# Four channel sums per round as two rounded products each, and the key norm at the end of the round before

## The reference

```python
kk = k * k_k.reshape(hs)
kk = kk / jnp.maximum(jnp.linalg.norm(kk, axis=-1, keepdims=True), 1e-12)      # key norm
...
var = jnp.mean(jnp.square(y - mu), axis=-1, keepdims=True)                      # variance of the output
y = (y - mu) * lax.rsqrt(var + B_LN_EPS) * ln_g.reshape(hs) + ln_b.reshape(hs)
y = y + jnp.sum(r * k * r_k.reshape(hs), axis=-1, keepdims=True) * v            # bonus
...
oa = _rmsnorm(_hgrn2(qa, fa, ia, lb), hg_norm.reshape(A_HEADS, A_HEAD_DIM))     # norm of the HGRN2 output
```

## Time and profile before

| | |
|---|---|
| runs before | 1185.59, 1187.63, 1187.63 us; median 1187.63 |
| the profiled execution | 1185.91 us, span from first to last instruction 1184.1 us |
| granted TensorE clock | 0.996 of full speed |
| TensorE busy | 1148.4 us (97%) |
| VectorE, Pool, ScalarE busy | 760.6 us (64%), 631.1 us (53%), 446.6 us (38%) |

### The profile page before, as it was taken

One profiled execution on the slowest core, in us unless ns is written; L12 is line 12 of the kernel. 1 busy time (PEld: TensorE's weight loads), 2 busy tenths in 40 slices (PEclk: granted clock), 3 DMA queues, 4 the chain that ended last, 5 costly groups with the idle time before them and its releaser, 6 DMA issues.

```text
span 1184.1 us, 31046 instructions
## 1 busy us (share of the span) xinstructions
PE 1148.4 (97%) x12076; PEld 907.4 (77%) x12076; DVE 760.6 (64%) x1339; ACT 446.6 (38%) x844; POOL 631.1 (53%) x594
## 2 busy tenths in 40 slices
PE   7899999999999999999999999998999999999996
PEld 4678877777788788777887878886677777778884
DVE  7874684675666746755766541638568686968637
ACT  5452343342533432434335410225234344453224
POOL 5553452442444524434444667876557474749872
PEclk9999999999999999999999999999999999999999
DMA  6221221221221212212112143333223222313331
GB/s 199 75 70 48 55 70 35 66 55 41 63 56 55 65 40 62 66 38 65 56 46 72 48 148 114 95 98 89 80 64 89 72 83 68 89 63 91 106 89 71
DMA packets 46890, 87.38 MB, mean 74 GB/s; under 512 B 5824, under 2 KB 7104, under 8 KB 46656
## 3 DMA queue, kind: packets, MB, share of 16 engines
q1 hardware_dynamic: 44496, 81.04, 23.4%
q10 hardware_dynamic: 2288, 4.72, 1.2%
HBM read 83.65 MB, written 2.10 MB: 72 GB/s over the span
## 4 chain that ended last, share of the span: by engine, by line
PE 80%; DVE 10%; ACT 3%; issue 2%; DVEq 0%; ACTq 0%
PE psum L398 77%; ACT mix L1175 2%; DVE mix L1733 2%; PE psum L1079 1%; DVE mix L2398 1%; PE psum L550 1%; DVE mix L2385 1%; DVE mix L2376 1%; DVE mix L2396 1%; DVE h_split L1737 1%; DVE mix L2486 0%; DVE psum L1853 0%; DVE psum L2287 0%; PE psum L712 0%; PE psum L548 0%
## 5 line engine op out<-in xcount | busy, mean ns | idle before, releaser
L398 PE MATMUL psum<-h_split,w_hi 128*128 128x512 f32 x2320 | 751.0, 405 | 17.5 <-DVE h_split L1733 8.2
L398 PEld LDWEIGHTS psum<-h_split,w_hi 128*128 128x128 f32 x2320 | 421.7, 189 | 124.8 <-issue 32.1
L352 POOL TENSOR_SCALAR w_hi<-w_raw 128x512 fp32r<-128x512 f32 x290 | 211.1, 728 | 492.8 <-PE psum L398 348.0
L398 PE MATMUL psum<-h_split,w_lo 128*128 128x512 f32 x1160 | 454.8, 392 | 0.0
L354 POOL TENSOR_TENSOR w_lo<-w_raw,w_hi 128x512 fp32r<-128x512 f32 x290 | 408.3, 1408 | 24.2
L1175 ACT ACTIVATE mix<-psum 128x512 f32<-128x512 f32 (+4 forms) x292 | 140.8, 496 | 384.6 <-PE psum L398 252.8
L398 PEld LDWEIGHTS psum<-mix 64*64 64x64 f32 (+3 forms) x8256 | 229.0, 138 | 70.6 <-issue 48.8
L398 PE MATMUL psum<-mix 64*64 64x64 f32 (+5 forms) x8256 | 270.1, 236 | 5.4 <-issue 2.4
L398 PEld LDWEIGHTS psum<-h_split,w_lo 128*128 128x128 f32 x1160 | 218.5, 188 | 47.7
L1175 ACT ACTIVATE mix<-mix 128x512 f32<-128x512 f32 (+3 forms) x256 | 131.4, 547 | 118.7 <-DVE mix L2268 48.0
L1853 DVE COPY_PREDICATED mix<-mask,psum 128x128 f32<-128x128 uint8 (+1 forms) x192 | 82.0, 469 | 44.2 <-PE psum L398 41.8
(11 more groups left out here) (136 smaller groups left out, 666.9 us busy)
## 6 DMA issues: line engine op xcount, KB each, us to landing
w_raw<-wall SPq DMA_DIRECT2D x290, 256.0 KB, 2.6
mix<-xT SPq DMA_DIRECT2D x4, 512.0 KB, 6.9
mix<-xT ACTq DMA_DIRECT2D x1, 2048.0 KB, 8.0
out<-mix SPq DMA_DIRECT2D x7, 256.0 KB, 2.5
mix<-pT ACTq DMA_DIRECT2D x2, 512.0 KB, 3.6
mix<-lru_w ACTq DMA_DIRECT2D x4, 256.0 KB, 3.1
mix<-w2a ACTq DMA_DIRECT2D x16, 32.0 KB, 2.3
mask<-mask_u SPq DMA_DIRECT2D x1, 432.0 KB, 7.5
```

What stands on the lines that cost most here:

```text
L352: pool.tensor_scalar(w_hi[:, slot, :, :], w_raw[:, slot, :], 1.0, 0.0, ALU.mult, ALU.add).then_inc(sem["w_hi"], 1)
L398: return pe.matmul(o, lhsT, rhs, start=start, stop=stop, skip_group_check=True)
```

## The change

Each of the four sums of a round becomes two products of fp32r type: the rounded (high) half of the operand, then the low half, both against rounded constants, added in the same bank. The last round's variance sum stays one fp32 matmul.

- The high halves are made by ScalarE (a second Square or a Copy with an fp32r output), the low halves by Pool (full minus high), at fixed places between its splits: output square behind the fourth unit of a round, bonus product behind the fifth, variance behind the fifteenth, keys behind the sixteenth. Pool's loop now runs over rounds, with 16 splits written out.
- The three halves that share `sum_split[:, 0]` (key, output square, bonus) take turns: ScalarE waits for the sum before.
- The key sum on TensorE moves from the beginning of a round to the end of the round before, between t(7) first half and `hg_level` 6; VectorE's clamp moves to the place ahead of `states`; ScalarE's Ln and Exp of it move ahead of the decay Exps. `low_rank`, which writes the same bank, waits for the clamp.
- In the last round the HGRN2 norm moves to the middle of tile 3.
- To make room in SBUF, `n_add`, `s_all`, `t2` and the odd layer's `osig` now share memory with other tiles. Two semaphores that nobody waits for are gone.

```diff
+        sum_split = sb("sum_split", [P, 2, 2, T], F32R)
+        sum_const = sb("sum_const", [P, 2, P], F32R)
+        ones_r, bones_r = sum_const[:, 0, :], sum_const[:, 1, :]
...
+            def key_low(r):
+
+                pool.wait_ge(sem["sum_hi"], count("sum_hi", r, 0))
+                pool.tensor_tensor(sum_split[:, 0, 1, :], t1, sum_split[:, 0, 0, :].bitcast(F32), ALU.subtract).then_inc(sem["sum_lo"], 1)
...
+            def variance_low(r):
+
+                pool.wait_ge(sem["rw_dsq"], count("rw_dsq", r))
+                pool.tensor_tensor(sum_split[:, 1, 1, :], y_sq, sum_split[:, 1, 0, :].bitcast(F32), ALU.subtract).then_inc(sem["dsq_lo"], 1)
+
+            pool.wait_ge(const_loaded, 64)
+            pool.tensor_scalar(sum_const[:, :, :], fconst[:, 1:3, :], 1.0, 0.0, ALU.mult, ALU.add)
...
+            with pool.Fori(1, EV_ROUNDS) as i:
+                for g in range(groups):
+                    for slot in range(SLOTS):
+                        split_unit(i * groups + g, slot)
+                        if g == 0 and slot == 3:
+                            output_square_low(i - 1)
+                        elif g == 1 and slot == 0:
+                            bonus_low(i - 1)
+                        elif g == 3 and slot == 2:
+                            variance_low(i - 1)
+                key_low(i)
...
+            def sum_products(o, of, pair):
+
+                mm(o, of, sum_split[:, pair, 0, :], True, False)
+                return mm(o, of, sum_split[:, pair, 1, :], False, True)
...
             def key_norm(r):
-                pe.wait_ge(sem["rw_ksq"], count("rw_ksq", r))
+                pe.wait_ge(sem["sum_lo"], count("sum_lo", r, 0))
+                sum_products(R0[:, :], bones_r, 0).then_inc(sem["rw_ssq"], 1)
...
             def bonus(r):
-                pe.wait_ge(sem["rw_rk"], count("rw_rk", r))
-                pe.wait_ge(sem["rw_m1"], count("rw_m1", r))
-                mm(R0[:, :], bones, t2).then_inc(sem["rw_bon"], 1)
...
             def hg_norm(r):
-                pe.wait_ge(sem["hg_sq"], count("hg_sq", r))
-                mm(H0[:, :], ones, hk).then_inc(sem["hg_ssq"], 1)
+                pe.wait_ge(sem["sum_lo"], count("sum_lo", r, 1))
+                sum_products(H0[:, :], ones_r, 0).then_inc(sem["hg_ssq"], 1)
...
                 t(7, 0, 4)
+                key_norm(i)
                 hg_level(i, 6)
...
                 low_rank(r)
-                part_tile(EV_ROUNDS, 3, 0, KC)
-                key_norm(r)
+                part_tile(EV_ROUNDS, 3, 0, 4)
                 hg_norm(r)
+                part_tile(EV_ROUNDS, 3, 4, KC)
                 head_var(r - 1)
                 bonus(r)
...
             def out_squares(r):
                 act.wait_ge(sem["rw_yc"], count("rw_yc", r))
...
+                    if not is_first(r):
+                        act.wait_ge(sem["rw_var"], count("rw_var", r - 1))
+                    f(by_parity(sum_split[:, 1, 0, :].rearrange("p (c t) -> p c t", c=RC)),
+                      psum[:, 2:4, 256:512].rearrange("p g (c t) -> p g c t", c=4), ACT.Square).then_inc(sem["rw_dsq"], 1)
...
+            def bonus_high(r):
+                act.wait_ge(sem["rw_rk"], count("rw_rk", r))
+                act.wait_ge(sem["hg_ssq"], count("hg_ssq", r))
+                f(sum_split[:, 0, 0, :], t2, ACT.Copy).then_inc(sem["sum_hi"], 1)
...
                     act.preload_act_table_set("natural_log_exp_and_others")
+                    key_scale(r)
...
                     if is_first(r):
                         decay_rates()
-                    act.wait_ge(sem["rw_m1"], count("rw_m1", r))
-                    f(t1, t1, ACT.Ln).then_inc(sem["rw_ln"], 1)
-                    act.wait_ge(sem["rw_ln"], count("rw_ln", r))
-                    f(t1, t1, ACT.Exp, bias=bias[:, 2:3], scale=-0.5).then_inc(sem["rw_rn"], 1)
+                    bonus_high(r)
...
-                f(t1, wk, ACT.Square, scale=cur_e[:, K_K:K_K + 1]).then_inc(sem["rw_ksq"], 1)
+                f(t1, wk, ACT.Square, scale=cur_e[:, K_K:K_K + 1])
+                if pair:
+                    act.wait_ge(sem["rw_bon"], count("rw_bon", r))
+                f(sum_split[:, 0, 0, :], wk, ACT.Square, scale=cur_e[:, K_K:K_K + 1]).then_inc(sem["sum_hi"], 1)
...
                 f(hk, H1[:, :], ACT.Square).then_inc(sem["hg_sq"], 1)
+                act.wait_ge(sem["rw_ssq"], count("rw_ssq", i))
+                f(sum_split[:, 0, 0, :], H1[:, :], ACT.Square).then_inc(sem["sum_hi"], 1)
...
                 if pair:
                     decay_sums(r)
-                    key_norm(r)
                     operands(r)
                     read_operands(r)
...
                 masked(i, 7)
+                key_norm(i)
                 states(i)
```

More of the change, by code:

```diff
@@ L50 @@
 SLOTS = 4
+MIX = 26700
 OUT_EARLY = (0, 1, 4, 5, 6, 2, 3, 7)
@@ L174, in place @@
             used[0] += width
-            assert used[0] <= 28800, used[0]
+            assert used[0] <= MIX, used[0]
             return mix[:, at:at + width]
@@ L195, in trunk @@
         shift = place(T + 8)
-        t1, t2, w_a = (place(T) for _ in range(3))
+        t1, w_a = (place(T) for _ in range(2))
+        t2 = kr[:, 0, :]
         cum = place(RC * (RL + 1)).rearrange("p (c t) -> p c t", c=RC)
@@ L505, in key_norm, with head_var, bonus @@
             def key_norm(r):
-                pe.wait_ge(sem["rw_ksq"], count("rw_ksq", r))
-                pe.wait_ge(sem["rw_sw"], count("rw_sw", r))
[L508 to L515, removed]
-                mm(R1[:, :], bones, y_sq).then_inc(sem["rw_var"], 1)
-            def bonus(r):
-                pe.wait_ge(sem["rw_rk"], count("rw_rk", r))
-                pe.wait_ge(sem["rw_m1"], count("rw_m1", r))
-                mm(R0[:, :], bones, t2).then_inc(sem["rw_bon"], 1)
+                pe.wait_ge(sem["sum_lo"], count("sum_lo", r, 0))
+                sum_products(R0[:, :], bones_r, 0).then_inc(sem["rw_ssq"], 1)
+            def head_var(r):
+                if isinstance(r, int) and r == EV_ROUNDS - 1:
+                    pe.wait_ge(sem["rw_dsq"], count("rw_dsq", r))
+                    pe.wait_ge(sem["rw_s"], count("rw_s", r, 5))
+                    last = mm(R1[:, :], bones, y_sq)
+                else:
+                    pe.wait_ge(sem["dsq_lo"], count("dsq_lo", r))
+                    pe.wait_ge(sem["rw_av"], count("rw_av", r + 1))
+                    last = sum_products(R1[:, :], bones_r, 1)
+                last.then_inc(sem["rw_var"], 1)
+            def bonus(r):
+                pe.wait_ge(sem["sum_lo"], count("sum_lo", r, 2))
+                pe.wait_ge(sem["rw_sw"], count("rw_sw", r))
+                sum_products(R0[:, :], bones_r, 0).then_inc(sem["rw_bon"], 1)
             def token_rows(r, n, head):
```

62 lines of the change are left out of this document (40 added, 22 removed).

## The result

The changed kernel takes **1197.72 us** in the median of four runs (1194.62 to 1198.89), against 1186.61 us of the kernel before beside it (1184.02 to 1187.63): ratio 1.0092 [1.0069, 1.0115], so 11 us slower. Six further runs of the changed kernel in a later series gave 1197.29 us, against 1186.14 us of 18 runs of the kernel before, ratio 1.0085 [1.0069, 1.0102]. The direction was forecast; the size (4.6 us) was less than half of it, and the time lies 0.7 us above the range. The profiled executions differ by 13.0 us (1198.89 to 1185.91).

A forecast was written before the change was run, and what follows sets the result against it. TensorE, busy 97%, was taken as the bound, with VectorE close behind in the head. Round terms 0.45 - 1.15 + 4.5 + 0.8 gave +4.6 us on the 1187.6 median: 1192.2 us, range 1180 to 1197.

The forecast's parts named there:

- The sum: Whole kernel: round 0 +0.45, round 1 -1.15, rounds 2 to 7 +4.5, last round +0.8, in total +4.6 us.
- the last round, put at +0.8 us: Before the first embedding tile: Pool's bonus half delays the bonus sum and the embedding halves; tile 0.8 us late (0.6 to 1.2).
- the regular rounds: Rounds 2 to 7: each loses 0.3 us in the head and 0.455 for the key sum at its end, +4.5 together.
- A sum costs 0.88 on TensorE, two products 0.455: TensorE's sums: each one made two rounded products saves 0.425 us; 31 of them take 13.2 us off TensorE.
- Pool holds VectorE, and the head gives the saving back: Round's head: Pool's added subtractions delay VectorE, so TensorE loses its whole 2.15 us saving and 0.3 more.
- The walk: VectorE and Pool in the head, step by step with hold prices: gating ends at 568.1 (566.41 before), masked copies 578.3 (577.48).
- Where TensorE waits: Just before the first inverse step: TensorE waits for the bonus, then gate product and masked copies, some 2 us per round.
- Round 1 at -1.15 us: Round 1: VectorE's 2.51 us wait ahead of the gate lets TensorE keep 1.6 us; with the key sum back, -1.15.
- The first rival: Masked copies end in time and TensorE stays the only bound: only the last round's loss remains, -10.2, 1177.4 us; chance 0.12.
- it evens out: The head gains 0.45 us, what the key sum at the round's end costs: no change, 1187.7 us; chance 0.16.
- serialises in full: Every Pool instruction of the head holds VectorE fully: head +1.3 us a round, +11 in total, 1198.6 us; chance 0.10.

The follow-up runs named there:

- version 1: Changed kernel without Pool's low halves of output square and bonus; each sum's second product rereads the high half (wrong values): 1180.51 us.
- version 3: Changed kernel with the output norm's and bonus's sums back as single fp32 sums, without halves: 1181.49 us.
- 2: Changed kernel with VectorE's gating of q moved ahead of the read operands: 1199.74 us.
- 9: Changed kernel; in the last round alone, output norm's and bonus's sums are fp32 without halves, the norm's sum behind the whole partial tile: 1192.39 us.
- version 11: Changed kernel with output norm's and bonus's sums in fp32 and, in the last round, the norm's sum behind the whole partial tile: 1178.99 us.
- version 4: Changed kernel with all four sums back in fp32, keeping only the early key norm: 1186.47 us.
- version 5: Changed kernel with the output norm's sum back in fp32; the bonus's low half stays on Pool: 1190.87 us.

## Why the prediction was right and wrong

The mechanism of the head (Pool's halves hold VectorE, and TensorE waits for it) was right, the place of the wait was not. The sum failed at two steps: the last round, put at +0.8 us, cost 3.9, and the sum had no term for half clock and issue waits, which the traces put at 4.6 us in the even rounds. Luck is in it too: the regular rounds were put 2.3 us too high, which hid a part of the rest.

- **A sum costs 0.88 on TensorE, two products 0.455: right.** By the starts of equal products a regular round's head gets shorter at the sums by 2.05 us in the changed trace (0.88 + 3 x 0.425 = 2.15 forecast), round 1's, which has no variance sum, by 1.65 (1.7 forecast), and each round gets 0.47 back at its end.
- **Pool holds VectorE, and the head gives the saving back: right, and shown** by 1 and 3. The walk put the gating at 568.1, 13.18 us after the scan's start; measured 13.20. The four multiplies ahead of it end within 0.1 us of the walk too, so this is no luck. Behind it the walk was too slow: the gate product ends 21.08 us after the scan's start, not 21.6. The price of a whole subtraction (1.16 us of VectorE's busy time) is in 1. The Trainium skill (GPSIMD Engine Reference, Specifications) speaks of shared SBUF interfaces for VectorE instructions with two SBUF inputs; the scan (1.24 to 1.63) and the multiplies lengthen, the gating from PSUM stays at 0.68: it agrees.
- **Where TensorE waits: wrong.** The step "It finds the bonus late ..., then the gate product and the masked copies" overlooked that t(2) needs the bank that the gating frees. TensorE arrives 11.68 us after the scan's start and the gating ends at 13.20; the wait was to be had from the prediction's own numbers (t(2) began at 568.51 before, less 2.15 is 566.4, and the walk's gating ended at 568.1). With the gating moved (2) the waits are where I had put them. The head of a regular round saves 2.05 us and gives 1.85 back at this place (1.58 of them idle), so it comes out 0.1 to 0.2 us ahead, not 0.3 behind. With the key sum's 0.47 such a round costs 0.3 to 0.4 us instead of 0.755: six of them 2.2 instead of 4.5. This term was too high.
- **Round 1 at -1.15 us: wrong.** It waits for the gating too (2.13 us in round 1's head, 87.81), and comes out 0.9 longer. The 2.51 us that VectorE waits at the gate product lie behind that place.
- **The last round at +0.8 us: mis-sized, the largest term.** By the starts of equal products it cost 3.9 us: 0.5 for the norm's sum in the middle of the tile, 1.0 net at the sums and the two waits, 1.6 of half clock, 0.7 at the issue wait at 689.81, which the second trace does not have (3.1 us there), and small rests. The wait for Pool's bonus half was named but left without its price (0.97); the embedding's halves (3.6 to 3.7 us from the last tile to the first embedding product, in the kernel before and in versions 3, 9 and 11) were covered by four sums of 0.88 before and by two pairs of products now, since the key sum and the norm's sum stand ahead of the tile's end; and half clock followed. Undoing the round alone gave 5 us (9).
- **Not in the sum at all: clock and issue waits.** The granted clock was 1.00 throughout the round, and I took every product at 0.227 us. The two stretches of half clock in rounds 2 and 3 are, with the issue waits, what these rounds cost beyond a regular one. The waits that the profile puts down to "issue" between 100 and 610 us add up to 6.3 and 5.8 us in the two traces of the changed kernel, 4.0 and 3.5 in those of before, 2.4 in version 11, 1.6 in version 4, but 6.0 in version 1, which has no late gating. They stand at the same few places of the code in all of them; why they are longer in some **stays open**, and no run was made that tells it.
- The first rival (TensorE alone is the bound) fell by 11.8 us of waits; "it evens out" fell by the same; "serialises in full" (1198.6) came nearest in time but for other reasons: the regular rounds cost less than forecast, and the rest came from the last round, the clock and the issue waits.

Together: rounds 0 and 1 0.7 us, the regular cost of rounds 2 to 7 6 x 0.37 = 2.2, issue waits 6.3 - 4.0 = 2.3, the two half-clock stretches of even rounds 2.3 (what is left of the 7.5 us up to the last scan; by the starts of equal products they take 1.5 each, so 0.7 came back at other places), last round 3.9, odd layer 1.4 (chance), 0.2 unplaced: 13.0.

## What to carry to other kernels

On a kernel bound by one engine, walk the head against the engine that frees its PSUM banks: for each tile note who reads the bank last, and how much later it may end. Work given to Pool is not free for a VectorE that is busy with SBUF inputs (here 1.2 us for a subtraction of 512 columns), so take such halves only where VectorE has room: the two sums in the second half of the round brought 5 us, the two in its head cost 16, and without their halves on Pool (version 1) they would still have brought only 1.0. When a sum is made shorter, ask also what it covered, and let the long form stand where it hides another engine's work, as the version that beats both kernels does.

## What I had not expected of the hardware

- TensorE falls to half clock behind some idle times and not behind others. It did not behind the regular waits of 1.58 us, the 1.71 us at 426.44, the 2.07 us in version 3's last round and the 2.22 us in version 5's (behind one of 0.35); it did behind 1.60 us at 282.26 (but not behind the 1.60 us at 279.35 in the kernel before), behind two of the three waits of 1.78 us in round 2, 2.46 us in version 1's last round, 0.97 and 2.21 us close together (all three traces that have both) and in or behind those of 3.44 us and more. So the length of one idle time doesn't tell it. The Trainium skill (Advanced Engine Details and Errata, Clock Domains) says that the array's clock is gated to 1.2 GHz when idle; these rows agree in so far as each such stretch of the even rounds and the last round stands in or behind an idle time, and they show the price here: a product of 0.227 us takes 0.43.
- Two subtractions on Pool hold VectorE hardly longer (2.38 us) than the bonus's alone (2.05).
- A subtraction put on VectorE itself cost its chain 1.7 us (6.04 - 4.35), not the 0.69 that it takes alone: between the 1.42 and 2.05 us that one on Pool cost.
